# Spreading the query projections over other tiles of a PEER sweep on one Trainium2 core

## The reference, cut to what matters

```python
def _peer(h, w_q, subkeys, u, v):
    ht = h.reshape(t, dm)                                     # t = 512 tokens, dm = 2048
    q = (ht @ w_q).reshape(t, PEER_HEADS, 2, PEER_HALF)       # 8 heads, 2 halves of 128
    sc = jnp.einsum("thcd,hckd->thck", q, subkeys)
    s1, i1 = lax.top_k(sc[:, :, 0], PEER_TOPK)                # 16 of 128
    s2, i2 = lax.top_k(sc[:, :, 1], PEER_TOPK)
    cand = (s1[..., :, None] + s2[..., None, :]).reshape(t, PEER_HEADS, 256)
    top, idx = lax.top_k(cand, PEER_TOPK)
    ...                                                       # expert numbers, softmax gates
    act = gelu(einsum("tkd,td->tk", u[experts], h)) * gates
    return einsum("tk,tkd->td", act, v[experts])
```

## Time and profile before

| | |
|---|---|
| median of 3 runs | 3014.53 us (3007.47 to 3015.68) |
| the profiled execution | 3011.45 us, span 3009.6 us, granted clock 0.993 |
| PE busy / PEld busy | 2917.9 us (97%) / 2599.8 us (86%) |
| DVE / ACT / POOL busy | 2319.1 us (77%) / 1048.3 us (35%) / 1488.0 us (49%) |
| chain that ended last, by engine | PE 71%, DVE 11%, DMA 11%, issue 3%, ACT 2% |

### The profile page before, as it was taken

The page is one execution under the profiler, slowest core; times in us unless marked ns, Lnnn a source line. Parts: engine busy times, 40 slices in busy tenths (PEclk is TensorE's granted clock), DMA queues, the critical chain, the costliest instruction groups (busy, mean ns, idle before and its releaser), DMA issues.

```text
span 3009.6 us, 40778 instructions
## 1 busy us (share of the span) xinstructions
PE 2917.9 (97%) x15249; PEld 2599.8 (86%) x15249; DVE 2319.1 (77%) x2974; ACT 1048.3 (35%) x1373; POOL 1488.0 (49%) x906
## 2 busy tenths in 40 slices
PE   7999999999999999999999999999999999999998
PEld 6888777778889999999999999999997877777787
DVE  5434677754588888988888887798777988898898
ACT  4121433341323333434333343333323433333343
POOL 1000222300015656565564654566768878788672
PEclk9999999999999999999999999999999999999999
DMA  7777777777458998989899898899999999999999
GB/s 257 259 246 216 231 242 239 221 273 259 137 185 293 326 329 298 348 305 330 299 325 328 296 352 280 301 328 330 340 348 393 414 414 414 412 409 417 415 415 364
DMA packets 321775, 947.11 MB, mean 315 GB/s; under 512 B 62484, under 2 KB 179232, under 8 KB 232288
## 3 DMA queue, kind: packets, MB, share of 16 engines
q1 hardware_dynamic: 177040, 475.04, 43.8%
q0 software_dynamic: 107008, 439.75, 40.8%
q10 hardware_dynamic: 37584, 30.43, 3.1%
HBM read 849.56 MB, written 95.55 MB: 314 GB/s over the span
## 4 chain that ended last, share of the span: by engine, by line
PE 71%; DVE 11%; DMA 11%; issue 3%; ACT 2%; SPq 0%; ACTq 0%; DVEq 0%; POOL 0%
PE ps L1737 22%; PE ps L1739 21%; PE ps L1738 21%; DMA v_raw<-in_peer_v 8%; PE ps L1987 4%; DMA wc_raw<-in_w_in 2%; DVE v_lo L1637 2%; DVE x_rows L1595 1%; DVE u_row L1586 1%; ACT v_hi L1116 1%; DVE x_one L1687 1%; DVE uT_lo L1575 1%; PE ps L1837 1%; DMA u_tile<-uT_all 1%; DVE seg_turned L1237 1%
## 5 line engine op out<-in xcount | busy, mean ns | idle before, releaser
L1737 PE MATMUL ps<-hT_hi,uT_hi 128*128 128x384 f32 x2048 | 700.8, 342 | 15.4 <-DVE uT_lo L1575 13.5
L1739 PE MATMUL ps<-h2T_lo,uT_hi 128*128 128x384 f32 x2048 | 687.0, 335 | 0.0
L1738 PE MATMUL ps<-hT_hi,uT_lo 128*128 128x384 f32 x2048 | 685.6, 335 | 0.0
L761 POOL DMA_INDIRECT gate_grid<-gates,grid_cells x256 | 518.6, 2026 | 107.5 <-issue 78.8
L1737 PE MATMUL ps<-v_hi,a_hi 128*128 128x512 f32 x1024 | 403.3, 394 | 37.1 <-DVE v_lo L1637 36.5
L1737 PEld LDWEIGHTS ps<-hT_hi,uT_hi 128*128 128x128 f32 x2048 | 385.4, 188 | 21.9 <-DVE uT_lo L1575 17.3
L1116 ACT ACTIVATE v_hi<-v_raw 128x2048 fp32r<-128x2048 f32 x128 | 245.6, 1919 | 454.2 <-PE ps L1739 329.7
L1738 PE MATMUL ps<-v_hi,a_lo 128*128 128x512 f32 x1024 | 401.5, 392 | 0.0
L1739 PE MATMUL ps<-v_lo,a_hi 128*128 128x512 f32 x1024 | 401.4, 392 | 0.0
L1738 PEld LDWEIGHTS ps<-hT_hi,uT_lo 128*128 128x128 f32 x2048 | 385.6, 188 | 1.9
L1739 PEld LDWEIGHTS ps<-h2T_lo,uT_hi 128*128 128x128 f32 x2048 | 384.8, 188 | 0.0
(11 more groups left out here) (206 smaller groups left out, 4982.7 us busy)
## 6 DMA issues: line engine op xcount, KB each, us to landing
v_raw<-in_peer_v SPq DMA_DIRECT2D x128, 1024.0 KB
u_tile<-in_peer_u SPq DMA_DIRECT2D x88, 1024.0 KB
seg_rows<-in_peer_u SPq DMA_DIRECT2D x40, 1024.0 KB, 6.4
u_tile<-uT_all SPq DMA_DIRECT2D x40, 1024.0 KB
uT_all<-seg_turned SPq DMA_DIRECT2D x100, 256.0 KB, 6.5
w_raw<-in_w_in SPq DMA_DIRECT2D x24, 1024.0 KB, 7.6
wc_raw<-in_w_in SPq DMA_DIRECT2D x48, 512.0 KB, 7.2
gate_grid<-zeros POOLq DMA_DIRECT2D x16, 1024.0 KB
```

What stands on the lines that cost most here:

```text
L761: pool.indirect_dma_start(out=gate_grid, out_offset=bass.IndirectOffsetOnAxis(ap=grid_cells[:, d, col:col + 1], axis=0), in_=gates[:, 2 + ...
L1737: mm(out, a_hi, b_hi, start=first, stop=False)
L1738: mm(out, a_lo, b_hi, start=False, stop=False)
L1739: return mm(out, a_hi, b_lo, start=False, stop=last)
```

## The change

Three of the six constants move work of head i + 2 to other tiles of the sweep, two more follow, and `QUERIES` becomes a list of tiles. In each of the first six sweeps:

| | before | after |
|---|---|---|
| PE, quarters of the first query half | end of tiles 3, 4, 5, 6 | 2, 4, 6, 8 |
| PE, quarters of the second | 9, 10, 11, 12 | 10, 11, 12, 13 |
| PE, keys transposed | 7 | 8 |
| PE, key scores | 8 and 14 | 10 and 14 |
| ACT, high parts of the weights | 1 and 7 | 1 and 9 |
| DVE, low parts of the weights | 2 and 8 | 2 and 10 |
| ACT, query copied out | 7 and 13 | 9 and 14 |
| SP, weights loaded | 0 and 5 | 0 and 5 |

No instruction is added or removed.

```diff
-SPLIT_WQ = (1, 7)
-QUERIES = (3, 9)
-KEYS_TURNED = 7
-QUERIES_OUT = (7, 13)
-KEY_SCORES = (8, 14)
+SPLIT_WQ = (1, 9)
+QUERIES = ((2, 4, 6, 8), (10, 11, 12, 13))
+KEYS_TURNED = 8
+QUERIES_OUT = (9, 14)
+KEY_SCORES = (10, 14)
 WQ_LOADS = (0, 5)
...
                         for c in range(2):
-                            if 0 <= b - QUERIES[c] < 4:
-                                queries(i + 2, c, b - QUERIES[c])
+                            if b in QUERIES[c]:
+                                queries(i + 2, c, QUERIES[c].index(b))
                             if b == KEY_SCORES[c]:
                                 score_keys(i + 2, c)
```

## The result

The changed kernel takes **3114.6 us** (median of 4 runs, 3111.89 to 3119.95) against 3012.0 for the kernel before, run beside it: 1.0337 times as long, 95% interval 1.0323 to 1.0352, or 102.6 us more. The prediction said 3113. Two slow executions, of 7542 us (the kernel before) and 4906 us (the one with both weight halves first), are left out of the ratios, but not of the medians; without its own the latter's 3038.3 would be 3036.5.

A forecast was written before the change was run, and what follows sets the result against it. PE sets the sweep's pace, with only some 15 to 20 us of waits to win. The profiled 3011.45 us plus 75.1 of new waits and 26.8 of lost clock gave 3113 us (+3.3%), range 3082 to 3132.

The forecast's parts named there:

- The three waits: PE waits for wq_ready in tile 2 (6.20 us) and tile 10 (5.32), for pqT_ready in tile 14 (3.9).
- The sum of the waits: Over six sweeps: 23.8 in tile 2, 31.0 in tile 10, 22.5 in tile 14, less 2.2 given back: 75.1 us.
- Its 5.31: Sixth sweep, tile 2: PE's wait for the weight split, 5.31 us, adding 4.68 us net.
- its 4.44: Sixth sweep, tile 10: PE's wait for wq_ready, 4.44 us, since a tile is 0.88 longer there.
- Tiles without a quarter: Tiles 3, 5, 7, 9 lose their quarter; DVE does not fall behind, costed at nothing.
- What is given back: PE, held in tile 14, waits less than the old 1.08 us in tile 1, in four sweeps: half taken, -2.2 us.
- The clock: Granted clock drops behind the new waits: 26.8 us, bounds 0 and 50; 2.1 us per wait over 5 us.
- the seven put at 3.0 to 4.4: Waits of 3.0 to 4.4 us: half counted as dropping the clock, at 1.5 us each, 5.3 us in all.
- The first rival: Sweep: the waits come but the clock stays up, 3087 us; chance 0.15.
- the second (every wait, 3128): Sweep: all 18 waits drop the clock, 42 us in place of 27, so 3128 us; chance 0.12.
- Faster (2994): Sweep: DVE runs ahead, the split is ready, quarter 0 swallows present waits in tiles 3 and 1: 2994 us; chance 0.03.
- The dense stage: Rival: order does not bind; split not waited for, or DMA-paced dense stage after the sweep absorbs losses: 3012 us; chance 0.02.

The follow-up runs named there:

- the one with both weight halves first: Changed kernel with both weight halves at the start of DVE's step, the second no longer behind the choice: 3038.3 us, ratio 1.0088 to the kernel before.
- the filled kernel: Changed kernel with useless matmuls put ahead of the three new waits (30 in tile 2, 25 in tile 10, 17 in tile 14): 3085.7 us.
- the spread without waits: Kernel before with first quarters in 3, 4, 6, 8, second in 10 to 13, second split in 8, key scores in 10 and 15: 3006.4 us.
- the kernel that removes the cause: Kernel before with each head's first weight split moved into the sweep ahead, quarters from tile 0, first sweep's order kept: 2997.2 us, ratio 0.9950.
- the kernel with the wait in tile 10 alone: Kernel before with weight split in tile 9, second quarters in 10 to 13, key scores in 10 and 15, second query copied in 14: 3050.7 us.
- the kernel with the wait in tile 14 alone: Kernel before with only the copy of the second query moved from tile 13 to 14: 3042.0 us, ratio 1.0100.
- the three with one wait each: Kernel before with only the new wait in tile 2, 10 or 14: 3043.2, 3050.7 and 3042.0 us.

## Why the prediction was right

**The three waits.** The mechanism is the one forecast, in each of its three places. Step by step, the third sweep: tile 2, 6.20 said, 6.17 measured; tile 10, `wq_ready` at T9 + 15.15 said, 15.15 measured (1385.52 - 1370.37), a wait of 5.3; tile 14, the copy done at T14 + 3.62 said, 3.35 measured, so a wait of 3.6 for 3.9 (in the fifth sweep alone it was 3.9). The copy starts 0.21 after the activation ahead of it, before that one's 0.29 are over; and that activation itself came at T14 + 2.56, where it was T14 + 2.75 in the row used, probably because the dot product it reads was ready (not shown). The sum of the waits was 75.1; filled with matmuls they cost 74. In the filled kernel T14 to T15 is 13.8, where the sum had 14.0.

**The sixth sweep was mis-summed.** The prediction let PE reach the wait in tile 2 at T2 - 0.20 and that in tile 10 0.88 later than in the other sweeps. But in that sweep 8 transposes stand behind each tile ahead of the wait, besides those that make the tile 0.88 longer; the prediction counted them for tile 14 alone. Its 5.31 was 4.42, its 4.44 was 3.55, and 1.8 us of the 75.1 are too much.

**Why it could be read.** Nothing on DVE or ACT ahead of the events that PE now waits for depends on where PE's quarters stand, so their times in the trace of before could be carried over. That held in every sweep, the sixth too: there `wq_ready` came at T2 + 5.05 and T9 + 15.15, as said. In the first sweep both the new wait and the old one in tile 2 are 0.9 longer than in the others, so the net cost is the same. The row for tile 10 was from another step (2 in place of 10), of the same kind.

**Tiles without a quarter.** Costed at nothing: in the first five sweeps tiles 4 to 9 of the changed kernel are at 9.22, 11.99 and 12.2, and the spread without waits lost nothing.

**What is given back.** 2.2 us said as half of what was possible; 10.30 to 9.55 in tile 1 of four sweeps is 3.0.

**The clock.** 26.8 us said, 28.9 measured, nearer 31 with the fills' excess. It was the least certain term, and its parts were less exact than its sum. Ten waits were over 5 us, not eleven; the eleventh, in tile 2 of the sixth sweep, was 4.4, and the clock fell there too. Of the seven put at 3.0 to 4.4 I let half drop the clock, 5.3 us in all; it fell at all five in tile 14 of the first five sweeps, at 1.3 to 2.9 each (15.11 to 16.68 for T14 to T15, against 13.8 or 14.1 filled), which is 10.1, and not at the two in the sixth of 3.37 and 2.53.

What a fall costs goes by how much of the low stretch lies behind the wait. The stretches last 3.4 us (five times) or 6.8 (eleven). In tile 10 the two short ones cost 1.5 and 1.6 and the three long ones 2.7 or 2.8; in tile 2 all six are long, but in sweeps 2 to 4 half of each lay inside the wait, and they cost 1.5 (T2 to T3 19.8 for 18.3), against 2.1 to 2.4 in the other three. The first rival (no falls, 3087) is what the filled kernel shows, 3086; the second (every wait, 3128) took two falls too many, and 2.4 us for each where 28.9 over 16 falls is 1.8 (2.0 by the tile lengths, below). On the Trainium skill's description (TensorE: Matmul & The Clock Gate, section on HAM oscillation), in which each wait between groups is followed by a slow start, this case comes close to it without being it: 16 of 18 waits fell.

**What was luck.** The total is within 2 us, but its terms are not as good. Added up from the lengths of the tiles in the profiled executions, the waits cost about 72 us where 75.1 was said (1.8 too much in the sixth sweep, 0.3 in five of the tiles 14, less 0.8 more given back), and the 16 falls about 32 where 26.8 was said. That the two errors cancel is chance.

**The other rivals.** Faster (2994) did not happen, by the reason given: in step 2 DVE has no idle time but some 0.15 us at a time between instructions of its own that depend on each other. Its size was right for the kernel that removes the cause (2997). The dense stage absorbed next to nothing: it is as long as before within 5 us.

## What to carry to other kernels

When work is moved ahead in one engine's queue, take the last event it needs from the old trace, and subtract the moment at which that engine will now ask: if nothing ahead of that event depends on the moved work, the difference is the new wait, to a few tenths of a microsecond. Count for each kind of tile by itself what the engine still does ahead of the wait: 8 transposes overlooked in one sweep made two of the waits here 0.9 too long. Look at the instruction that increments the semaphore, not at the step that it belongs to: here the first half of the weights was ready 5.7 us before the second, which alone counted, and moving that one forward took back 76 of 103 us. Add to each wait of TensorE what the granted clock loses behind waits of its length in the same trace.

## What the runs showed of the hardware

The clock's loss can be had back without removing a wait: 432 useless matmuls made the kernel 29 us faster, since the granted clock stayed at 1.00. And the length of the idle time alone does not say whether the clock falls. It stayed at 1.00 after 3.37 us in tile 10 of the sixth sweep of the changed kernel, and fell to 0.73 over 6 us after the same 3.37 in the same tile of the kernel with the wait in tile 10 alone. In the first sweep it fell after 2.44 us in the kernel before and stayed at 1.00 after 2.44 in the kernel with the wait in tile 14 alone. In one kernel it fell after 1.80 us in the third sweep and not after 1.79 in the second, with the same work around both. At every wait of 3.43 us or more in the sweep it fell, in the changed kernel and in the three with one wait each. What decides at the shorter ones stays open.
